# Second mixer: gate tiles through Silu on their way out of PSUM, gated and split beneath the last tiles, and the first two output tiles in the same stage

## The chip, the core and the metric

The kernel runs on one core of one Trainium2 chip. A core has a matrix engine (TensorE, PE in the rows; its weight loads are PEld), a vector engine (VectorE, DVE), an activation engine (ScalarE, ACT), GpSimd (POOL) and a sync engine that issues the DMAs (SyncE, SP). Each engine works through its own queue in order, and they meet through semaphores. The metric is the device time of one execution in microseconds; less is better.

## The reference, cut to what matters

Two blocks follow each other. The first is two layers of mixer and feed-forward and takes most of the time; the change does not touch it. The second block is one mixer layer on 512 tokens of 1024 features:

```python
proj = jnp.einsum('btd,de->bte', rmsnorm(x, pre_norm_g), w_in)
q_a, f_a, i_a, g_a, u_b, g_b, q_c, k_c, v_c, g_c, f_c = jnp.split(proj, IN_SPLIT_POINTS, axis=-1)
o_a = rmsnorm(hgrn2(silu(q_a), ...), hgrn_norm_g) * silu(g_a)   # 256 features
o_b = pooled(u_b) * pool_scale * silu(g_b)                      # 256 features
o_c = forgetting_attention(q_c, k_c, v_c, log_f_c) * silu(g_c)  # 512 features, 8 heads
mixed = jnp.concatenate([o_a, o_b, o_c], axis=-1)
y = jnp.einsum('bte,ed->btd', mixed, w_out)
out = x + rmsnorm(y, post_norm_g)
```

Everything is float32. The large products are made from parts: weight and activation are each split into a high part of type fp32r and a low rest, and three products (high by high, high by low, low by high) are summed in PSUM.

## The kernel before

The whole program is a row of stages. Each stage is one block in which every engine has its own written list of instructions; at a stage's end all engines meet (line 99), and no engine starts the next stage before all have come. The last two stages are `second_mix` and `finish`.

**`second_mix`** makes 28 dense tiles of 128 features by 512 tokens, j = 0 to 27, two for each weight unit u. Tile j is 24 matmuls: 8 slices of the contraction, kt, by 3 products. They go into the first bank of `ps0` or `ps1`. A unit of weights (1 MB) lands in one of four `raw` slots; ACT makes its high part (`split_hi`, line 158) and DVE its low part (`split_lo`, line 165) in one of two slots. The units are ordered by `SEC_COLS`: the last four units, tiles 20 to 27, are the gates g_a, g_b and g_c, and line 3574 copies these out of PSUM into `gate`, untouched.

Beneath the dense tiles lies the rest of the mixer. Behind slices 2, 5 and 7 of each tile PE calls a hook, `beside(j, x)` with x = 0, 1, 2, and ACT and DVE have the same hooks in their lists. From tile 17 on each hook holds one step i of the attention, `fox(i)`, 32 steps in all (2 groups of 4 heads, 4 chunks of queries, 4 heads). Step i on PE: the scores of i (line 3935), the transposes of the probabilities of i-1 (3945), the products with the values of i-2 (3955), and every fourth step the transposes of a finished chunk (3963). On DVE: row maximum and sum with the bias (3800), its negative (3804), every fourth step the division (3808, 3813). On ACT: the exponential of step i (3590), then the copy of the transposed probabilities of i-1 (3597), every fourth step the copy of a finished chunk into `mix` (3602). So PE needs in the next hook what ACT makes in this one. ACT's copy of a dense tile (`leave(j)`) stands behind the hook x = 2, its `split_hi` behind the hook x = 0 of every second tile, DVE's `split_lo` behind x = 1.

Tile 27 ends with step 32. Steps 33 and 34 (the `rest` list) stand behind it, then `split_hi` and `split_lo` of the second output unit and the load of ACT's function table for Silu (line 3674). The first output unit has been split in tile 26.

**`finish`** multiplies the gates by the mixer's values, splits the product into `ahi` and `alo`, multiplies by `w_out` in 8 output tiles of 24 matmuls (`one`, line 4163), takes the gain, transposes each tile to token layout (`y_turn`, 4172), and squares it for the norm; the residual `h` is transposed in 8 groups of four transposes (`h_turn`, 4154), groups 0 and 1 ahead of the tiles and six among tiles 2 to 4. For the first two tiles slices alternate between the tiles, and each slice waits for its `alo` (4115), which comes from a chain by slice: Silu on ACT (4073), product on DVE (4120), high part on ACT (4076), low part on DVE. At the end come the sums of squares (4195, 4198), the inverse root on ACT, eight fused multiply-adds (4145) and the output DMAs.

Of the kernel before, what the change touches and what calls it, by code (L numbers as in the profile page):

```python
# [23 lines left out]
P = 128  # L24
# [2293 lines left out]

def gdn(k, ins, ctx, late):
# [1093 lines left out]
def second_mix(k, cols, lower, hgrn_gain, f_cols, f_bias, pool_w, pool_scale, mix, gate, then):  # L3413
# [22 lines left out]
    with ExitStack() as ctx:  # L3436
        sb = lambda nm, shape: ctx.enter_context(nc.sbuf_tensor(f"sm_{nm}", shape, F32))
        kc = sb("kc", [P, 4, SEQ])
        ba, qa = sb("ba", [P, 4, SEQ]), sb("qa", [P, 2, SEQ])
        st, lev = sb("st", [P, 2, 2, NCH, CH]), sb("lev", [P, LEVELS, CH // 2])  # L3440
        vt, kt = sb("vt", [P, NCH, 2, P]), sb("kt", [P, 2, NCH, P])
        s2, nb = sb("s2", [P, NCH - 1, 2, P]), sb("nb", [P, FH, SEQ])
# [33 lines left out]
                 "o_ready", "inverse", "o_done", "o_turned", "out_done")  # L3476
# [21 lines left out]
        def _(sp):  # L3498
# [3 lines left out]
            with nc.allow_non_contiguous_dma(reason="256 bounds and gains, feature on partitions"):  # L3502
                sp.dma_start(lx[:, :], lower[0].rearrange("(t p) -> p t", p=P)).then_inc(s.lx_in, 16)
                sp.dma_start(hgain[:, :], hgrn_gain.rearrange("(t p) -> p t", p=P)).then_inc(s.hgain_in, 16)
            gates.sync(k, sp)
            pooling.sync(k, sp)
            for j in range(nj):
# [6 lines left out]
                if j == 9:  # L3514
                    sp.wait_ge(s.negc_out, 16)
                    sp.wait_ge(s.scanned, 1)
                    for h in range(FH):
                        sp.dma_start(nb[:, h, :], k.negc_d.ap()[h:h + 1, :].to_broadcast([P, SEQ])).then_inc(s.nb_in, 16)
            k.loaded = len(then)
# [31 lines left out]
        def _(act):  # L3551
# [3 lines left out]
            def leave(j):  # L3555
# [48 lines left out]
            def beside(j, x):  # L3604
# [44 lines left out]
                if j >= FOX0:  # L3649
                    fox(fox_at(j, x))  # L3650
            def split(j):
# [19 lines left out]
            for i in rest:  # L3671
                fox(i)
            split_hi(k, act, u0 + SECN + 1, ring(SECN + 1), t0 + nj)
            nc.scalar.preload_act_table_set("silu_and_others")

        @block.vector
        def _(dve):
# [114 lines left out]
            def fox(i):  # L3792
# [12 lines left out]
                if i % 4 == 1 and i >= 5:  # L3805
# [5 lines left out]
                    if n >= 2:  # L3811
                        dve.wait_ge(s.o_turned, n - 1)
                    dve.tensor_tensor(o[:, n % 2, :, :], bank_a[0][:, 0:4 * HW].rearrange("p (h d) -> p h d", d=HW),
                                      sm[:, n, :].unsqueeze(2).to_broadcast([P, 4, HW]), ALU.mult).then_inc(s.o_done, 1)
            def beside(j, x):
# [34 lines left out]
                if j >= FOX0:  # L3850
                    fox(fox_at(j, x))
            def split(j):
# [10 lines left out]
            for i in rest:  # L3863
                fox(i)
            split_lo(k, dve, u0 + SECN + 1, ring(SECN + 1))

        @block.tensor
        def _(pe):
# [155 lines left out]
            for i in rest:  # L4024
                fox(i)
# [5 lines left out]
def finish(k, gate, value, gain_row, out):  # L4031
# [10 lines left out]
    with ExitStack() as ctx:  # L4042
        sb = lambda nm, shape, dt=F32: ctx.enter_context(nc.sbuf_tensor(f"fin_{nm}", shape, dt))
        ahi, alo = sb("ahi", [P, KD, SEQ], F32R), sb("alo", [P, KD, SEQ], F32R)
        a, yg, sq, sqs = sb("a", [P, 2, SEQ]), sb("yg", [P, 2, SEQ]), sb("sq", [P, 2, SEQ]), sb("sqs", [P, SEQ])
        gain, rinv = sb("gain", [P, KD]), sb("rinv", [P, NCH])
        ht, yt = sb("ht", [P, NCH, D]), sb("yt", [P, NCH, D])
        names = ("gain_in", "gated", "scaled", "a_hi", "a_lo", "gained", "squared", "pooled", "y_turned", "y_out", "h_turned",
# [12 lines left out]
        def _(sp):  # L4061
            with nc.allow_non_contiguous_dma(reason="1024 gains, feature on partitions"):
                sp.dma_start(gain[:, :], gain_row.rearrange("(k p) -> p k", p=P)).then_inc(s.gain_in, 16)
# [6 lines left out]
        def _(act):  # L4070
            for kt in range(KD + 1):
                if kt < KD:
                    nc.scalar.activation(gate[:, kt, :], gate[:, kt, :], ACT.Silu).then_inc(s.gated, 1)  # L4073
                if kt > 0:
                    act.wait_ge(s.scaled, kt)
                    nc.scalar.copy(ahi[:, kt - 1, :], a[:, (kt - 1) % 2, :]).then_inc(s.a_hi, 1)  # L4076
            nc.scalar.preload_act_table_set("natural_log_exp_and_others")
# [34 lines left out]
        def _(dve):  # L4112
            def low(kt):
# [159 lines left out]
```

## Time and profile before

| | us |
|---|---|
| median of 3 runs | 1951.26 |
| lowest and highest of these | 1950.52, 1952.03 |
| the profiled execution, its own time | 1950.78 |
| its span, first to last instruction | 1949.0 |
| PE busy in the span | 1873.5 (96%) |
| DVE, ACT busy | 1058.5 (54%), 871.7 (45%) |

The rows further down come from that profiled execution, and times in them count from the start of its span. A row of a timeline gives start and duration. PE is pipelined, so its rows overlap: what a matmul costs in a stream is the distance from its start to the next one's start, not the duration in its row. A bracket at the end of a row says how long the engine had been idle before it and what ended that; a Q behind an engine's name is its sequencer, and L99 the meeting of the engines between stages.

### The profile page before, as it was taken

Reading aid. Unit: us, or ns where it says so; the run is one execution under the profiler, and the core shown is the slowest. Engines: PE = TensorE matmul, PEld = TensorE weight load, DVE = VectorE, ACT = ScalarE, POOL = GpSimd, SP = SyncE. Lnnn points to the kernel's source line nnn. Section 1 sums busy time; section 2 is a strip of 40 time slices with the busy share of each in tenths; the row PEclk is TensorE's granted clock in tenths of the full one; section 3 lists DMA queues with packets and bytes.
Section 4 is the critical chain, followed back from the end, with each engine's and each line's share of the span. In section 5 each row is a group of like instructions: output and inputs, shape, how many; then the busy total and the mean of one; then the engine's idle time right before and its main releaser. Section 6 shows DMA issues by size and latency. Waiting matters only on the chain. (4 is left out here: it accounts for less than half of the span.)

```text
span 1949.0 us, 31267 instructions
## 1 busy us (share of the span) xinstructions
PE 1873.5 (96%) x12700; PEld 1679.9 (86%) x12700; DVE 1058.5 (54%) x1724; ACT 871.7 (45%) x1449; POOL 109.4 (6%) x142
## 2 busy tenths in 40 slices
PE   7999999999899999999989999999999998999988
PEld 7999999899699999999989877788888885787666
DVE  6666599976733444444452276454443447863343
ACT  6557763667723433333343366342322333424452
POOL 0001150000000000000000020000000002001101
PEclk8999999999999999999989999999999998999989
DMA  8223362254432222322222233223223222321201
GB/s 200 85 78 126 118 191 74 62 159 138 121 92 83 87 88 94 100 87 86 86 67 88 69 78 95 87 87 108 86 90 104 86 86 67 113 66 40 65 1 44
DMA packets 209631, 179.34 MB, mean 92 GB/s; under 512 B 42544, under 2 KB 181808, under 8 KB 209512
## 3 DMA queue, kind: packets, MB, share of 16 engines
q1 hardware_dynamic: 209512, 177.68, 30.5%
q8 instruction: 83, 1.36, 0.3%
q14 instruction: 36, 0.29, 0.0%
HBM read 164.10 MB, written 13.54 MB: 91 GB/s over the span
## 5 line engine op out<-in xcount | busy, mean ns | idle before, releaser
L165 DVE TENSOR_TENSOR main_wlo<-raw,main_whi 128x2048 fp32r<-128x2048 f32 x98 | 225.7, 2303 | 328.4 <-ACT main_whi L158 328.4
L158 ACT CAST main_whi<-raw 128x2048 fp32r<-128x2048 f32 x98 | 186.5, 1903 | 368.5 <-PE ps L196 368.5
L196 PE MATMUL ps<-ffn_xhi,main_whi 128*128 128x264 f32 (+1 forms) x768 | 206.8, 323 | 6.6 <-DVE ffn_xlo L697 6.6
L196 PE MATMUL ps<-ffn_xlo,main_whi 128*128 128x264 f32 (+1 forms) x768 | 206.7, 323 | 0.0
L196 PE MATMUL ps<-ffn_xhi,main_wlo 128*128 128x264 f32 (+1 forms) x768 | 206.4, 323 | 0.0
L196 PE MATMUL ps<-ffn_alo,main_whi 128*128 128x264 f32 (+1 forms) x768 | 205.8, 322 | 0.0
L196 PE MATMUL ps<-ffn_ahi,main_wlo 128*128 128x264 f32 (+1 forms) x768 | 205.1, 321 | 0.0
L196 PE MATMUL ps<-ffn_ahi,main_whi 128*128 128x264 f32 (+1 forms) x768 | 204.7, 321 | 0.0
L196 PE MATMUL ps<-gdn_xhi,gdnf_whi 128*128 128x264 f32 x768 | 160.4, 290 | 4.2 <-DVE gdnf_wlo L1248 4.2
L196 PE MATMUL ps<-gdn_xlo,gdnf_whi 128*128 128x264 f32 x768 | 156.2, 285 | 0.0
L196 PE MATMUL ps<-gdn_xhi,gdnf_wlo 128*128 128x264 f32 x768 | 156.0, 284 | 0.0
L196 PEld LDWEIGHTS ps<-ffn_xhi,main_whi 128*128 128x128 f32 x768 | 128.9, 190 | 19.1 <-issue 7.4
L196 PEld LDWEIGHTS ps<-ffn_xlo,main_whi 128*128 128x128 f32 x768 | 128.5, 189 | 11.6 <-issue 0.2
L196 PEld LDWEIGHTS ps<-ffn_xhi,main_wlo 128*128 128x128 f32 x768 | 128.4, 190 | 11.0
L196 PEld LDWEIGHTS ps<-ffn_ahi,main_whi 128*128 128x128 f32 x768 | 127.8, 188 | 11.6
L196 PEld LDWEIGHTS ps<-ffn_alo,main_whi 128*128 128x128 f32 x768 | 127.5, 188 | 11.2
L196 PEld LDWEIGHTS ps<-ffn_ahi,main_wlo 128*128 128x128 f32 x768 | 127.5, 188 | 10.9
L380 DVE TENSOR_TENSOR h<-h,ps 128x528 f32<-128x528 f32 (+1 forms) x128 | 85.6, 691 | 81.2 <-PE ps L196 81.2
L196 PEld LDWEIGHTS ps<-gdn_xhi,gdnf_whi 128*128 128x128 f32 x768 | 120.7, 190 | 5.6 <-DVE gdn_xlo L1235 4.5
L196 PEld LDWEIGHTS ps<-gdn_xlo,gdnf_whi 128*128 128x128 f32 x768 | 119.6, 189 | 0.0
L196 PEld LDWEIGHTS ps<-gdn_xhi,gdnf_wlo 128*128 128x128 f32 x768 | 119.2, 189 | 0.0
L1137 DVE SCALAR_TENSOR_TENSOR gdn_y<-gdnf_pre,gdnf_convw,gdn_y 128x528 f32<-128x528 f32 x96 | 82.5, 861 | 59.3 <-ACT gdn_y L1110 56.9
(518 smaller groups left out, 3687.4 us busy)
## 6 DMA issues: line engine op xcount, KB each, us to landing
raw<-in_ff_up_dram SPq DMA_DIRECT2D x32, 1024.0 KB, 5.4
raw<-in_ff_down_dram SPq DMA_DIRECT2D x32, 1024.0 KB, 5.0
raw<-in_gdn_in_dram SPq DMA_DIRECT2D x24, 1024.0 KB, 5.7
raw<-in_w_in_dram SPq DMA_DIRECT2D x14, 1024.0 KB, 5.3
raw<-in_mlstm_in_dram SPq DMA_DIRECT2D x12, 1024.0 KB, 5.4
raw<-in_gdn_out_dram SPq DMA_DIRECT2D x8, 1024.0 KB, 6.6
gdn_zr<-gdn_z_spilled SPq DMA_DIRECT2D x26, 264.0 KB, 3.2
gdn_v_spilled<-gdn_o SPq DMA_DIRECT2D x16, 264.0 KB, 2.2
```

The source lines that it names most:

```text
L158: k.nc.scalar.copy(k.whi[:, slot % SPLIT_SLOTS, :], k.raw[:, slot, :]).then_inc(k.hi_done, 1)
L165: eng.tensor_tensor(k.wlo[:, s, :], k.raw[:, slot, :], k.whi[:, s, :].bitcast(F32), ALU.subtract).then_inc(k.lo_done, 1)
L196: mm = pe.matmul(ps[:, b, 0:k.width], w, x[:, half], start=first and n == 0, stop=last and n == 2)
L380: dve.tensor_tensor(parted(k, acc[:, j, k.now]), parted(k, acc[:, j, k.now]), filled(k, k.ps[j % 4]), ALU.add).then_inc(s.down_free, 1)
L1137: dve.scalar_tensor_tensor(out=self.y[:, b, :], in0=self.pre[:, b, i:i + T], scalar=self.w[:, i, j:j + 1], in1=self.y[:, b, :], op0=ALU.mu ...
```

## The change

Four things are done together.

1. Tiles 20 to 27 leave PSUM through Silu instead of a copy. Silu lives in another function table than Exp and Ln, so a load of the table stands ahead of each Silu and another behind it.
2. The product with the mixer's values, the high part and the low part of slices 0 to 5 are made beneath the tiles that follow: for slice kt the product stands on DVE behind the hook x = 0 of tile 21 + kt, the high part on ACT behind x = 1, the low part on DVE behind x = 2. Slices 6 and 7 stand at the stage's end. The results lie in two buffers (`fin_first`, `fin_second`) placed over scratch of the stage that is free by then (`under_both`, `Gated`).
3. The first two output tiles move into `second_mix`, behind tile 27: slices 0 to 5 of tile 0, with steps 33 and 34 of the attention behind its slices 2 and 5, slices 0 to 5 of tile 1, then slices 6 and 7 of both.
4. `finish` starts with output tile 2. All eight groups of `h_turn` now stand among tiles 2 to 5. The DMA of the gains moves to the start of `second_mix`; the two table loads (lines 3674 and 4077) are gone.

```diff
@@ second_mix, SyncE
+                sp.dma_start(out_gain[:, :], gain_row.rearrange("(k p) -> p k", p=P)).then_inc(s.gain_in, 16)
@@ second_mix, ScalarE
-                    ins = nc.scalar.copy(gate[:, 2 * (u - 10) + m, :], src)
+                    ins = nc.scalar.activation(gate[:, j - SEC_GATE0, :], src, ACT.Silu)
                 ins.then_inc(s.left, 1)
+                if j >= SEC_GATE0:
+                    nc.scalar.preload_act_table_set("natural_log_exp_and_others")
+            def gated_high(kt_):
+                act.wait_ge(s.gated, kt_ + 1)
+                nc.scalar.copy(gated.hi(kt_), gate[:, kt_, :]).then_inc(s.gated_hi, 1)
...
+                if x == 1 and SEC_GATE0 < j <= SEC_GATE0 + 6:
+                    gated_high(j - SEC_GATE0 - 1)
...
             for i in rest:
                 fox(i)
+            for kt_ in range(6, KD):
+                gated_high(kt_)
             split_hi(k, act, u0 + SECN + 1, ring(SECN + 1), t0 + nj)
-            nc.scalar.preload_act_table_set("silu_and_others")
@@ second_mix, VectorE
+            def gated_product(kt_):
...
+                dve.wait_ge(s.left, SEC_GATE0 + kt_ + 1)
+                g = gate[:, kt_, :]
+                dve.tensor_tensor(g, g, mix[:, kt_, :], ALU.mult).then_inc(s.gated, 1)
+            def gated_low(kt_):
+                dve.wait_ge(s.gated_hi, kt_ + 1)
+                dve.tensor_tensor(gated.lo(kt_), gate[:, kt_, :], gated.hi(kt_).bitcast(F32), ALU.subtract)\
+                    .then_inc(s.gated_lo, 1)
...
+            gated_product(6)
+            gated_product(7)
+            gated_low(6)
+            gated_low(7)
             split_lo(k, dve, u0 + SECN + 1, ring(SECN + 1))
@@ second_mix, TensorE
-            for i in rest:
-                fox(i)
+            pe.wait_ge(k.lo_done, u0 + SECN + 1)
+            after = {2: rest[0], 5: rest[1]}
+            for j in range(2):
+                pe.wait_ge(s.left, nj - 1 + j)
+                for kt_ in range(6):
+                    pe.wait_ge(s.gated_lo, kt_ + 1)
+                    gated.tile(k, pe, j, kt_, u0 + SECN, dense[j])
+                    if j == 0 and kt_ in after:
+                        fox(after[kt_])
+            for kt_ in range(6, KD):
+                pe.wait_ge(s.gated_lo, kt_ + 1)
+                for j in range(2):
+                    gated.tile(k, pe, j, kt_, u0 + SECN, dense[j])
@@ finish, TensorE
-            for g in range(2):
-                h_turn(g)
-            pe.wait_ge(k.lo_done, u0 + 1)
-            for kt in range(KD):
-                pe.wait_ge(s.a_lo, kt + 1)
-                for j in range(2):
-                    one(j, kt)
             for j in range(2, 2 * n):
...
-                    if j < 5 and kt in (2, 5):
-                        h_turn(2 * (j - 1) + (2, 5).index(kt))
+                    if j < 6 and kt in (2, 5):
+                        h_turn(2 * (j - 2) + (2, 5).index(kt))
```

The order on PE where the two stages meet, before. `sm_ba` holds probabilities, `sm_qa` their transposes, `sm_s2` a finished chunk, `h` the residual:

```order
L196 MATMUL ps1<-sec_xhi,main_wlo 128x512
L3945 MATMUL ps2<-ident,sm_ba 128x128
L3955 MATMUL ps0<-sm_vt,sm_qa 128x64 x2
L3963 MATMUL ps1<-ident,sm_s2 128x128 x2
L99 UNCONDITIONAL_BRANCH
L4148 UNCONDITIONAL_BRANCH
L4154 MATMUL ps2<-ident,h 128x128 x4
L4154 MATMUL ps3<-ident,h 128x128 x4
L4163 MATMUL ps0<-fin_ahi,main_whi 128x512
```

The same place on PE in the change, from the last dense tile's end through the first six matmuls of output tile 0 and the step behind them:

```order
L196 MATMUL ps1<-sec_xhi,main_wlo 128x512
L4017 MATMUL ps2<-ident,sm_ba 128x128
L4027 MATMUL ps0<-sm_vt,sm_qa 128x64
L3443 MATMUL ps0<-fin_first,main_whi 128x512 x2
L3443 MATMUL ps0<-fin_first,main_wlo 128x512
L3443 MATMUL ps0<-fin_first,main_whi 128x512 x2
L3443 MATMUL ps0<-fin_first,main_wlo 128x512
L3443 MATMUL ps0<-fin_first,main_whi 128x512 x2
L3443 MATMUL ps0<-fin_first,main_wlo 128x512
L4027 MATMUL ps0<-sm_vt,sm_qa 128x64
```

The second product with the values moved behind nine matmuls, the transposes of the last chunk behind nine more, and the residual's transposes behind the meeting of the engines.

The order on ACT around the end of tile 26 (x = 2 there and x = 0 in tile 27), before:

```order
L3590 ACTIVATE sm_ba,wide<-sm_ba,wide 128x128
L3597 COPY sm_qa<-ps2 128x128
L3574 COPY wide<-ps0 128x512
L3590 ACTIVATE sm_ba,wide<-sm_ba,wide 128x128
L3597 COPY sm_qa<-ps2 128x128
L3602 COPY wide<-ps1 128x2x128
```

and in the change:

```order
L3634 ACTIVATE sm_ba,wide<-sm_ba,wide 128x128
L3641 COPY sm_qa<-ps2 128x128
L3613 ACT_TABLE_LOAD
L3613 ACTIVATE wide<-ps0 128x512
L3616 ACT_TABLE_LOAD
L3634 ACTIVATE sm_ba,wide<-sm_ba,wide 128x128
L3641 COPY sm_qa<-ps2 128x128
L3646 COPY wide<-ps1 128x2x128
```

Two loads now stand between the exponential of one hook and that of the next. On DVE the stage's end reads, in the change:

```order
L3855 RECIPROCAL wide<-wide 128x4
L3860 TENSOR_TENSOR sm_s2<-ps0,wide 128x256
L3874 TENSOR_TENSOR wide<-wide 128x512 x2
L3877 TENSOR_TENSOR fin_first<-wide,fin_first 128x512 x2
L165 TENSOR_TENSOR main_wlo<-raw,main_whi 128x2048
L99 UNCONDITIONAL_BRANCH
```

The low part of the weights (line 165) now stands behind the products and low parts of slices 6 and 7.

## Rows read from the trace of the kernel before

**Rows 1.** The page: busy time, share and instructions of each engine

```profile
PE 1873.5 (96%) x12700; PEld 1679.9 (86%) x12700; DVE 1058.5 (54%) x1724; ACT 871.7 (45%) x1449; POOL 109.4 (6%) x142
```

**Rows 2.** The chain that ended last, in `finish`: start, us, what

```profile
1885.68 15.84 PE ps L4163 x57
1901.52 0.44 PE ps L4154 x4
...
1904.93 3.50 PE ps L4163 x15
```

**Rows 3.** Timeline of PE from tile 27's last matmul to output tile 2

```profile
1875.66 0.39 PE L196 MATMUL ps<-sec_xhi,main_wlo 128*128 128x512 f32 x1
...
1877.53 0.44 PE L3963 MATMUL ps<-ident,sm_s 128*128 128x128 f32 x2 [0.57 <-DVE sm_s L3813]
1882.83 1.94 PE L4154 MATMUL ps<-ident,h 128*128 128x128 f32 x8 [4.86 <-PEq L99]
1885.68 0.76 PE L4163 MATMUL ps<-fin_ahi,main_whi 128*128 128x512 f32 x1 [0.92 <-DVE fin_alo L4115]
...
1899.26 0.40 PE L4163 MATMUL ps<-fin_ahi,main_whi 128*128 128x512 f32 x1
```

**Rows 4.** Timeline of ACT and DVE over the same seam

```profile
1876.20 0.27 ACT L3597 COPY sm_qa<-ps 128x128 f32<-128x128 f32 x1 [0.80 <-PE ps L3945]
...
1878.01 0.37 ACT L3602 COPY wide<-ps 128x256 f32<-128x256 f32 x1 [1.05 <-PE ps L3963]
1878.28 1.90 ACT L158 CAST main_whi<-raw 128x2048 fp32r<-128x2048 f32 x1
...
1880.21 2.29 DVE L165 TENSOR_TENSOR main_wlo<-raw,main_whi 128x2048 fp32r<-128x2048 f32 x1 [2.74 <-ACT main_whi L158]
...
1883.47 1.29 DVE L4120 TENSOR_TENSOR fin_a<-wide 128x512 f32<-128x512 f32 x2 [0.97 <-ACT wide L4073]
...
1884.19 0.62 ACT L4076 CAST fin_ahi<-fin_a 128x512 fp32r<-128x512 f32 x1 [0.24 <-DVE fin_a L4120]
...
1884.85 0.69 DVE L4115 TENSOR_TENSOR fin_alo<-fin_a,fin_ahi 128x512 fp32r<-128x512 f32 x1
```

**Rows 5.** Windows; behind the busy times stands PEclk, the granted clock

```profile
1885.60:1890.80 5.20, 5.12 (x12) 4.08 (x13) 4.84 (x8) 4.46 (x9) 0.00 (x0) 0.50 0.00 0
1890.80:1899.30 8.50, 8.50 (x38) 6.83 (x38) 5.35 (x9) 3.46 (x5) 0.00 (x0) 1.00 0.00 0
```

**Rows 6.** Timeline of PE at an earlier meeting of the engines

```profile
1202.30 0.39 PE L196 MATMUL ps<-mls_xhi,main_wlo 128*128 128x512 f32 x1
1203.02 0.70 PE L196 MATMUL ps<-mls_early,main_whi 128*128 128x512 f32 x2 [0.32 <-PEq L99]
1203.56 0.40 PE L196 MATMUL ps<-mls_early,main_wlo 128*128 128x512 f32 x1
```

**Rows 7.** Timeline of ACT around a table load for Silu, tile 4

```profile
1657.35 0.72 ACT L3376 ACTIVATE sm_nb<-sm_nb,ones 8x512 f32<-8x512 f32 x1
1658.09 1.28 ACT L3564 ACT_TABLE_LOAD   x1
1659.38 0.60 ACT L3564 ACTIVATE sm_qa<-ps 128x512 f32<-128x512 f32 x1
```

**Rows 8.** Timeline of ACT and PE between tiles 26 and 27

```profile
1868.93 0.58 ACT L3574 COPY wide<-ps 128x512 f32<-128x512 f32 x1
1871.60 0.40 ACT L3590 ACTIVATE sm_ba<-sm_ba,wide 128x128 f32<-128x128 f32 x1 [2.08 <-DVE wide L3804]
...
1874.12 0.33 PE L3945 MATMUL ps<-ident,sm_ba 128*128 128x128 f32 x1
...
1874.43 0.48 PE L196 MATMUL ps<-sec_xhi,main_whi 128*128 128x512 f32 x1
...
1874.75 0.39 PE L196 MATMUL ps<-sec_xlo,main_whi 128*128 128x512 f32 x1
```

**Rows 9.** Timeline of ACT and PE between tiles 22 and 23, widest steps

```profile
1825.13 0.58 ACT L3574 COPY wide<-ps 128x512 f32<-128x512 f32 x1
1827.55 0.72 ACT L3590 ACTIVATE sm_ba<-sm_ba,wide 128x512 f32<-128x512 f32 x1 [1.83 <-DVE wide L3804]
...
1831.31 0.66 PE L3945 MATMUL ps<-ident,sm_ba 128*128 128x128 f32 x4
```

More of the change, by code:

```diff
@@ L2316, in under, with under_both @@
         return t
+def under_both(k, first, second):
+    with k.nc.sbuf_tensor(*first, F32) as a, k.nc.sbuf_tensor(*second, F32) as b:
+        return a, b
 def gdn(k, ins, ctx, late):
@@ L3410, in second_unit, with __init__, room, hi @@
     return lambda u: tall(ins["w_in_2"][0], SEC_COLS[u])
-def second_mix(k, cols, lower, hgrn_gain, f_cols, f_bias, pool_w, pool_scale, mix, gate, then):
+class Gated:
+    def __init__(self, gate, value, first, second):
+        self.gate, self.value, self.first, self.second = gate, value, first, second
+    def room(self, kt, part):
+        if 4 <= kt < 6:
+            return self.second[:, 2 * (kt - 4) + part, :]
+        return self.first[:, 2 * (kt if kt < 4 else kt - 2) + part, :]
+    def hi(self, kt):
+        return self.room(kt, 0)
+    def lo(self, kt):
+        return self.room(kt, 1)
+    def tile(self, k, pe, j, kt, u0, bank):
+        u, m = u0 + j // 2, j % 2
+        x, cols = u % RAW_SLOTS % SPLIT_SLOTS, slice(m * P, (m + 1) * P)
+        whi = k.whi[:, x, :].rearrange("p (k n) -> p k n", k=KD)
+        wlo = k.wlo[:, x, :].rearrange("p (k n) -> p k n", k=KD)
+        for i, (w, y) in enumerate(((whi, self.hi(kt)), (whi, self.lo(kt)), (wlo, self.hi(kt)))):
+            mm = pe.matmul(bank, w[:, kt, cols], y, start=kt == 0 and i == 0, stop=kt == KD - 1 and i == 2)
+        if kt == KD - 1:
+            mm.then_inc(k.tile_full, 1)
+SEC_GATE0 = 20
+def second_mix(k, cols, lower, hgrn_gain, f_cols, f_bias, pool_w, pool_scale, mix, gate, st, nb, kt, kc, gated, out_gain,
+               gain_row, then):
     nc = k.nc
@@ L4028, in second_mix, with finish @@
     k.split = 2
-def finish(k, gate, value, gain_row, out):
+def finish(k, gated, gain, out):
     nc = k.nc
@@ L4070, in _ @@
         def _(act):
[L4071 to L4077, printed above, removed]
             def square(j):
@@ L4214, in second @@
                        w[:, 3584:3584 + FH], ins["fox_f_bias_2"][0], ins["pool_w_2"][0], ins["pool_scale_2"][0], mix, gate,
+                       st, nb, kt, kc, gated, gain, ins["post_norm_g_2"][0],
                        [tall(ins["w_out_2"][0], 256 * u) for u in range(4)])
-        finish(k, gate, mix, ins["post_norm_g_2"][0], out)
+        finish(k, gated, gain, out)
 _USED = ["x", "meta_tokens", "attn_norm", "ffn_norm", "ff_up", "ff_down", "gdn_in", "gdn_conv", "gdn_a_log",
```

67 lines of the change are left out of this document (29 added, 38 removed).

## The prediction

> **What bounds the kernel now.** The page comes first: PE is busy 96% of the span and no other engine over 54% [rows 1], so time goes away only where PE stands still, or runs below full speed, and an engine that gets more work costs nothing while PE does not wait for it. The chain of waits is read next for the stretch that the change touches: in `finish` it is nothing but PE's matmuls from 1885.68 on, 57 of them in 15.84 us [rows 2], so every microsecond by which this stream starts earlier ends the kernel earlier. Then the timeline of PE ahead of that chain. Tile 27's last matmul starts at 1875.66, output tile 2's first at 1899.26, 23.60 us later [rows 3]. Between them lie 48 matmuls of output tiles 0 and 1. In a stream of full speed 15 such matmuls take 3.50 us, 0.233 us each [rows 2], so 48 are 11.20 us. Half of the 23.60 us is something else, and the rows name it: 4.86 us idle until the engines meet, 0.92 us idle until the first slice's low part is there [rows 3], and a granted clock of 0.50, the 1.2 GHz level, until about 1890.8. The 12 matmuls in that window took 5.20 us and not 2.80, which is 2.4 us lost; from there on the clock is 1.00, 2.4 GHz [rows 5]. Ahead of the fall PE had stood for most of 5 us.
>
> What ends last at that meeting is DVE: `split_hi` 1.90 us, then `split_lo` 2.29 us until 1882.50 [rows 4]. Both belong to output tiles 2 and 3, which PE does not need yet.
>
> **The change, part by part.**
>
> *PE between 1875.66 and output tile 2.* In the change this reads: the last dense matmul 0.23; the small group of step 32; nine matmuls, the values of step 31, nine more, the transposes of the last chunk, 18 of tile 1, 12 of slices 6 and 7; the meeting of the engines. A small group costs, from its first row to the dense matmul behind it, 1874.43 - 1874.12 = 0.31 us, and the dense matmul then 0.32 rather than 0.23 [rows 8], so 0.40. Three of them are 1.20 us. The seam: where all other engines had come before PE, 0.72 us lay between the two matmuls' starts around the meeting [rows 6], 0.49 above a stream's 0.23. Sum: 0.23 + 1.20 + 11.20 + 0.49 = 13.12 us against 23.60. That is 10.48 us less, if PE waits for nothing and the clock stays.
>
> *The residual's transposes.* Groups 0 and 1 stood in time that was lost anyway; now they stand in PE's stream, 0.44 us each [rows 2]: 0.88 us more.
>
> *Does PE wait for the gated slices?* Slices 0 to 5 have their low parts one tile after their gates left, the last in tile 26; PE wants them after tile 27. Slices 6 and 7 are the narrow place. Their product needs the last chunk. By the sum above its transposes end at about 1881.3 on PE. Then, with durations from [rows 4]: copy on ACT 0.37 (1881.7); two products on DVE 1.29 (the first at 1882.4, both at 1883.0); high parts on ACT 0.62 each (1883.1, 1883.7); low parts on DVE 0.69 each, by about 1883.8 and 1884.5. PE wants slice 6 after 18 more matmuls, at about 1885.4, and slice 7 1.4 us later. The slack is 1.6 us; without that cover PE would stand 4 us there. The clock should stay up, since PE never stands for over half a microsecond.
>
> *Do the engines meet in time?* `split_hi` follows the high parts, 1883.7 + 1.90 = 1885.6, `split_lo` 2.29 more: 1887.9. PE's last matmul of slice 7 starts at about 1888.0 and the engines meet behind its end. DVE is there 0.3 us before PE. This is the thinnest cover; gone, it costs only what DVE is late.
>
> *What ACT pays for Silu.* Each gate tile's exit was a copy of 0.58. Now it is a load, Silu, a load. The trace has such a load beside its Silu: the load starts as the instruction before ends, takes 1.28 us, and Silu from PSUM starts 0.01 us behind it and takes 0.60 [rows 7]. So an exit takes 1.28 + 0.60 + 1.28 + 0.03 = 3.2 us instead of about 0.5, eight times, with a high part of 0.62 more in six of the tiles. Over 20 us more on ACT, all beneath PE's tiles, and the question is whether any of it reaches PE. Behind the exit of tile 26 ACT had 2.08 us idle until the next exponential [rows 8]. Exit from 1869.0 to 1872.2 puts that exponential 0.6 us late, its end with the copy behind it at 1872.8. PE wants it at 1874.12: slack 1.3 us. At the widest steps, behind tile 22, the exit would end at 1828.4, the exponential 0.9 us late, exponential and two copies done by 1830.2, and PE wants them from 1831.31 on [rows 9]: slack 1.1 us. The others lie between or better. I take 0 for the tiles; the upper bound is the rival below.
>
> *DVE's products and low parts* (0.69 each, six pairs) fall into idle time like the 2 us that [rows 8, 9] show on ACT; each follows the attention's step of its hook. Behind it only the next hook's step is queued, about 3 us later.
>
> *The DMA of the gains* moves ahead of the attention's gate weights and the pooling weights on SP; a 4 KB transfer, first used by PE two tiles later. 0.
>
> *`finish`* begins with gain, square and `split_hi` for output unit 2 as soon as the engines have met; its low part is wanted two tiles (over 13 us) later. 0.
>
> Sum: 10.48 - 0.88 = 9.6 us less. On the profiled execution's own 1950.78 us that is 1941.2. That execution lies 0.5 below the median of 1951.26; halfway between them, since the three runs themselves spread over 1.5 us, I say **1941.4 us**.
>
> **The rivals.**
>
> *A, the seam is not clean.* The low parts of slices 6 and 7 come later than PE, or DVE's `split_lo` makes the meeting late, PE stands, and the clock falls once more. Price: the standing (1 to 2 us) and the 2.4 us of the half clock [rows 5]. Gain 5 to 6: 1945.2. Against it: 1.6 us of slack, and a meeting of 0.72 us left the clock at full rate [rows 6].
>
> *B, a table switch costs more than its load.* If ACT lost a further 1.4 us per load, which the rows do not show (Silu 0.01 us behind the load [rows 7]), an exit would take 6.0 us. Behind tile 26 the exponential would start at 1875.0 instead of by 1874.12 less its 0.40: PE stands 1.3 us there, and by the same working 0 to 1.5 us behind the other six exits that a hook follows, some 6.5 us in all. Gain 3: 1948.0. The Trainium skill, "ScalarE: Activation LUTs", section "What ACT_TABLE_LOAD costs", gives each switch a load of about 1283 ns and on top of it a drain of about 1380 ns, 2.66 us in all; by that rule B is the forecast. The trace agrees on the load's length and shows no drain.
>
> *C, slower than before.* ACT's lateness reaches PE at the exits, and each time PE slows to 1.2 GHz for a stretch like that of [rows 5]: 2.4 us and the standing, some 3 us for each of the seven exits that a hook follows. It decides from the fourth exit on (9.6 / 3 = 3.2); all seven would be 21 us, 1962. For it: the work is put on ACT at seven places. Against it: it needs ACT over 1.1 us later than worked out at the tightest place, and pauses of a fraction of a microsecond between hooks do not lower the clock today.
>
> *D, it does not do what it says:* slices 0 to 5 are not ready beneath the tiles (a product waits for its gate tile with the attention's steps queued behind it on DVE), and the idle time only moves ahead of tile 27. Gain under 4: 1949.
>
> **How the numbers follow.** Forecast 0.80, A 0.08, B 0.06, C 0.03, D 0.03. Range 1939.8 to 1945.2: below, a seam and small groups at half their price (1 us) and the runs' own spread; above, A. A measurement of this kernel can tell about 0.2%, 3.9 us, from no change. Forecast and A are faster by more than that (0.88). B, 3.3 us below the median, and D lie within it, though B's sum is soft enough to put 0.02 of it on the faster side. C is slower: faster 0.90, same 0.07, slower 0.03.
>
> **What would show it.** Right: PE's row of output tile 2's first matmul 9 to 11 us earlier (near 1888.8), granted clock 1.00 through the seam, Exp rows behind the exits starting at most 1 us later while PE's transposes stay where they were. Wrong: a bracket with ACT or DVE on PE's rows in tiles 21 to 27 (B, C, D), a gap of over 1.5 us ahead of slice 6 or at L99 and matmuls 0.43 us apart behind it (A). A drain would be a gap between a load's end and the exponential behind it.

## The result, and the profile after

The changed kernel took **1935.88 us** (median of 4 runs, 1935.70 to 1939.68); the kernel before, in its runs beside it, 1950.89 (4 runs, 1949.47 to 1952.03). The ratio is 0.9928, 95% interval 0.9911 to 0.9945. The direction was forecast; the time lies 5.5 us below the forecast and 3.9 us below the range's low end. With all the runs of the experiments the picture changes: 26 runs of the changed kernel have a mean of 1939.8 us (1935.55 to 1947.63), 104 of the kernel before 1949.5 (1943.31 to 1957.31). The difference of the means is 9.8 us, with two standard errors 8.3 to 11.2. The four runs of the result lie low: of the other 22 runs of the same kernel only one is below 1935.88, and four drawn at random from all 26 have so low a median about once in 170.

The profiled execution after took 1935.70, its span is 1934.0, 15.0 shorter than before. First PE's line of the page, which answers [rows 1]: 7.1 us less busy. Of that 2.4 are the matmuls at the seam, which no longer run at 1.2 GHz, and 2.9 lie ahead of the second mixer (1565.5 us busy before, 1562.6 after), where nothing was changed.

```profile
PE 1866.4 (97%) x12700; PEld 1674.9 (87%) x12700; DVE 1059.8 (55%) x1724; ACT 886.6 (46%) x1455; POOL 107.0 (6%) x142
```

The timeline of PE from tile 27's last matmul to output tile 2, which answers [rows 3]; columns as there (L4017 are turns of probabilities, L4027 values, L4035 the chunk's transposes, L3443 the output tiles):

```profile
1870.60 0.39 PE L196 MATMUL ps<-sec_xhi,main_wlo 128*128 128x512 f32 x1
1870.83 0.27 PE L4017 MATMUL ps<-ident,sm_ba 128*128 128x128 f32 x1
...
1871.08 0.71 PE L3443 MATMUL ps<-fin_first,main_whi 128*128 128x512 f32 x2
1871.63 0.39 PE L3443 MATMUL ps<-fin_first,main_wlo 128*128 128x512 f32 x1
...
1873.26 0.33 PE L4027 MATMUL ps<-sm_vt,sm_qa 128*128 128x64 f32 x2
1873.40 0.72 PE L3443 MATMUL ps<-fin_first,main_whi 128*128 128x512 f32 x2
1873.95 0.39 PE L3443 MATMUL ps<-fin_first,main_wlo 128*128 128x512 f32 x1
...
1880.02 0.63 PE L3443 MATMUL ps<-fin_first,main_whi 128*128 128x512 f32 x2
...
1881.41 0.63 PE L3443 MATMUL ps<-fin_first,main_whi 128*128 128x512 f32 x2
...
1882.58 0.40 PE L3443 MATMUL ps<-fin_first,main_wlo 128*128 128x512 f32 x1
1883.30 0.70 PE L3443 MATMUL ps<-fin_first,main_whi 128*128 128x512 f32 x2 [0.33 <-PEq L99]
```

From 1870.60 to 1883.30 are 12.70 us; before they were 23.60, forecast were 13.12. The one bracket is the meeting of the engines, 0.33 us. The windows of this stretch and the next (PEclk is the third number from the right) answer [rows 5]:

```profile
1870.60:1883.30 12.70, 12.38 (x57) 9.74 (x56) 5.30 (x6) 6.83 (x8) 0.00 (x0) 1.00 0.00 0
1883.30:1890.80 7.50, 7.50 (x39) 6.18 (x40) 5.04 (x6) 3.58 (x4) 1.30 (x1) 1.00 0.01 2
```

The granted clock is 1.00 through the seam. ACT and DVE over the same stretch, which answers [rows 4]: tile 27's exit (load, Silu, load), the last chunk's copy, products, high and low parts of slices 6 and 7, and the split of output unit 2.

```profile
1871.42 1.28 ACT L3613 ACT_TABLE_LOAD   x1
1872.71 0.60 ACT L3613 ACTIVATE wide<-ps 128x512 f32<-128x512 f32 x1
1873.33 1.28 ACT L3616 ACT_TABLE_LOAD   x1
1876.01 0.37 ACT L3646 COPY wide<-ps 128x256 f32<-128x256 f32 x1 [1.39 <-PE ps L4035]
...
1876.41 1.29 DVE L3874 TENSOR_TENSOR wide<-wide 128x512 f32<-128x512 f32 x2 [2.30 <-ACT wide L3646]
1877.79 1.29 DVE L3877 TENSOR_TENSOR fin_first<-wide,fin_first 128x512 fp32r<-128x512 f32 x2
1880.20 2.29 DVE L165 TENSOR_TENSOR main_wlo<-raw,main_whi 128x2048 fp32r<-128x2048 f32 x1 [1.11 <-ACT main_whi L158]
```

The row of low parts (L3877) holds two of 0.69 us each: that of slice 6 is there at 1878.5, that of slice 7 at 1879.1. PE takes slice 6 at 1880.02 and slice 7 at 1881.41: 1.5 and 2.3 us of slack. DVE ends at 1882.49, and PE starts its last matmul ahead of the meeting at 1882.58. Last, ACT and PE behind the exit of tile 26, which answers [rows 8] and, for the load and its Silu, [rows 7]:

```profile
1864.19 1.28 ACT L3613 ACT_TABLE_LOAD   x1
1865.48 0.60 ACT L3613 ACTIVATE wide<-ps 128x512 f32<-128x512 f32 x1
1866.10 1.28 ACT L3616 ACT_TABLE_LOAD   x1
1867.39 0.40 ACT L3634 ACTIVATE sm_ba<-sm_ba,wide 128x128 f32<-128x128 f32 x1
...
1869.04 0.33 PE L4017 MATMUL ps<-ident,sm_ba 128*128 128x128 f32 x1
```

The exponential starts 0.01 us behind the second load. ACT takes its next copy into `mix` at 1867.94, 1.1 us before PE turns the result. At the widest steps, behind tile 22 [rows 9], the exponential starts at 1823.35, it and two copies are done at 1824.9, and PE wants them from 1826.21 on: 1.3 us.

**Where the 15.0 us of span lie.** Four stretches, whose ends are rows of the timelines: the start of the second mixer (its first DMA), tile 27's last matmul, the first transpose of the residual inside output tile 2 (2.1 to 2.2 us behind that tile's first matmul), and the span's end.

```profile
1619.36 0.37 SPq L3503 DMA_DIRECT2D sm_lx<-in_lower_bounds_dram  x1
```

```profile
1614.79 0.37 SPq L3540 DMA_DIRECT2D sm_lx<-in_lower_bounds_dram  x1
```

The first row is of before, the second of after. Before, the ends lie at 1619.36, 1875.66, 1901.36, 1949.0; after, at 1614.79, 1870.60, 1885.48, 1934.0. So 4.57 us were gained ahead of the second mixer, where nothing was changed; 0.49 in its tiles; 10.82 at the seam; and 0.88 were lost behind it. The edited part gives 9.94 us. The other 5.06 are the question.

### The profile page after: what moved, and what is told of

The parts are those of the page before. It is cut to its first block and busy times, and to the rows that moved or that the text cites. A ratio compares the mean times of both kernels' runs of the same rounds, so it can differ in the third digit from the quotient of the medians.

```text
span 1934.0 us, 31276 instructions
## 1 busy us (share of the span) xinstructions
PE 1866.4 (97%) x12700; PEld 1674.9 (87%) x12700; DVE 1059.8 (55%) x1724; ACT 886.6 (46%) x1455; POOL 107.0 (6%) x142
## 5 line engine op out<-in xcount | busy, mean ns | idle before, releaser
L196 PEld LDWEIGHTS ps<-ffn_ahi,main_whi 128*128 128x128 f32 x768 | 128.0, 188 | 11.6
L196 PEld LDWEIGHTS ps<-ffn_alo,main_whi 128*128 128x128 f32 x768 | 126.9, 188 | 11.2
```

Of the source, the lines that this page charges most:

```text
L196: mm = pe.matmul(ps[:, b, 0:k.width], w, x[:, half], start=first and n == 0, stop=last and n == 2)
```

## The experiments

Theory L (chance): the unchanged stages take another time in each execution, and the result caught a short one. Rival P (program): the changed program really speeds up what lies ahead of it. The runs were made in four groups, each on one chip and beside runs of the kernel before: same_before, same_after, beneath_only and extra_loads; same_before2, same_after2, silu_only and one_load; same_after3 and tail_split; one_extra. The ratios compare within a group.

### Both kernels again, unedited

> The kernel before, unchanged, run and profiled again. The two first profiles differ by 15.0 us in span, but only 9.9 us of that lie between tile 27's last matmul and the end; 4.6 us are there already when second_mix begins (engines released at 1619.2 us before, 1614.6 after), in stages whose code the change leaves alone. Theory L (lottery): those 4.6 us are a matter of the single execution, mostly of how long TensorE happens to be at 1.2 GHz in the earlier stages (34 us of such stretches before, 24 us after); this profile's second_mix then begins anywhere within 1614 to 1620 us and the times of this kernel spread over several us. Theory P (program): they belong to the program as built; second_mix begins at 1619 +- 1 us again and the median is 1951 +- 1 us.

> The changed kernel, unchanged, run and profiled again. Theory L (lottery): second_mix begins anywhere within 1614 to 1620 us, and the difference to the kernel before comes out nearer to 9.9 us than to 15. Theory P (program): second_mix begins at 1614.6 +- 1 us again, the median is 1936 +- 1 us and the difference is 15 us. Under both, the stretch from tile 27's last matmul to output tile 2's first takes 12.7 us and the stretch from there to the end 50.7 us.

> The changed kernel once more, nothing edited. Theory L (the local gain is fixed, about 9.9 us from tile 27's last matmul to the end, and what a single run shows beside that is chance in the stages that the change leaves alone): from tile 27's last dense matmul to output tile 2's first 12.70 us again within 0.1 and from there to the end of the span 50.7 within 0.3; median of the runs 1940 to 1943, ratio to before 0.994 to 0.996; the start of the second mixer anywhere between 1614 and 1621. Theory P (the changed program also speeds up what comes ahead of it, by code or buffers that lie elsewhere): median 1935 to 1937, start of the second mixer at 1615 or below.

> The kernel before once more, nothing edited. Theory L: the runs again spread over more than 8 us with a mean of 1949 to 1951, the long ones with the lower mean clock, about 1.5 us for each 0.001 (26 runs of it gave a slope of 1.45 us, correlation -0.84); from the last dense matmul to output tile 2's first 23 to 24 us. Theory P: second mixer's start at 1618 to 1620 every time.

> The changed kernel, nothing edited, as the neighbour of the version with the split tail and for more runs of it. From tile 27's last dense matmul to output tile 2's first 12.70 us, from there to the end 50.7; median 1938 to 1943; over all its runs and all of before's, means 9 to 11 us apart.

| run | median us (n) | ratio to before, 95% | mixer starts | last dense matmul | seam | behind it |
|---|---|---|---|---|---|---|
| before, first profile | | | 1619.36 | 1875.66 | 25.70 | 47.64 |
| same_before | 1948.03 (10) | 1.0002, 0.9988 to 1.0016 | 1617.78 | 1873.22 | 25.31 | 47.67 |
| same_before2 | 1948.69 (12) | 0.9997, 0.9984 to 1.0011 | 1618.99 | 1874.74 | 25.36 | 47.70 |
| after, first profile | 1935.88 (4) | 0.9928, 0.9911 to 0.9945 | 1614.79 | 1870.60 | 14.88 | 48.52 |
| same_after | 1941.94 (5) | 0.9959, 0.9941 to 0.9978 | 1618.98 | 1875.45 | 14.88 | 48.47 |
| same_after2 | 1939.45 (7) | 0.9956, 0.9938 to 0.9974 | 1617.11 | 1872.93 | 14.88 | 48.49 |
| same_after3 | 1938.84 (10) | 0.9950, 0.9935 to 0.9966 | 1621.10 | 1877.46 | 14.88 | 48.46 |

"Seam" is from tile 27's last matmul to the residual's transpose in tile 2, "behind it" from there to the end. These two columns repeat to 0.06 us within a kernel, before's seam apart (0.4). The start of the mixer moves over 1614.8 to 1621.1 with the same program, so P, which put it at 1615 or below every time, falls: the gain at the seam is the same in the slowest and in the fastest of these profiles, and the 4.57 us ahead of it come and go. L stands. From the mixer's start to the last dense matmul are 255.4 to 256.3 us in the three profiles of before and 255.8 to 256.5 in the four of the changed kernel, so the tiles with their new exits give nothing and cost at most some tenths. Of the numbers expected, the median of 1940 to 1943 for same_after2 missed (1939.45); the 23 to 24 us of same_before2 held (25.36 - 2.10 = 23.26), and the mean of its runs, 1949.2, fits.

What moves is in part the clock. Over the 67 runs of the kernel before in three of the groups the mean granted clock lay between 0.978 and 0.987; 15 runs at 0.982 had a mean of 1951.8 us, 10 at 0.985 one of 1946.7. The line through all has 1.2 us for each 0.001 (1.5 were expected), correlation -0.78. That is not all of it. Ahead of the mixer the records show 37.5 us at the half clock in before's first profile and 30.4 in after's; at half speed those 7.1 us cost 3.6 at most, of the 4.57. But over all 13 profiles of this study, in which this time was 30.4 to 47.5 us, the mixer's start follows it only loosely (correlation 0.47): same_after3, with 34.1, starts last. In before's and after's first profiles a part of the difference also stands as 0.13 us in each turn of the first block's first feed-forward loop, 23.49 against 23.36, at a granted clock of 1.00 in both; that is 1.3 us over ten turns. All 13 profiles have one of these two values. The changed kernel has 23.36 in three of its profiles and 23.49 in same_after3, silu_only has 23.36, and before had 23.49 in all three of its own. So it is not fixed by the program; what makes it was not found and stays open.

### The change without PE's new order

Everything of the change, but output tiles 0 and 1 stay in `finish`:

```diff
@@ second_mix, TensorE
-            after = {2: rest[0], 5: rest[1]}
-            for j in range(2):
...
-                    gated.tile(k, pe, j, kt_, u0 + SECN, dense[j])
+            for i in rest:
+                fox(i)
@@ finish, TensorE
-            for j in range(2, 2 * n):
+            for j in range(2 * n):
```

> The change without its third part: Silu at the exits and products, high and low parts beneath the tiles, but output tiles 0 and 1 stay at the start of finish, as whole tiles one after the other. Theory M (the gain is the overlap of the output tiles with the seam): the engines meet when DVE's split of the second output unit ends, which now stands behind the products of slices 6 and 7; about 9 us after tile 27's last matmul, and output tiles 0 and 1 follow with some 12 matmuls at 1.2 GHz. Worked out: 9.2 + 11.2 + 2.4 = 22.8 us from tile 27's last matmul to output tile 2's first, against 23.6 before and 12.7 in the change, so a gain of 0 to 1 us locally. Rival: the gated operands being ready is worth the most of the gain, then this is 5 us or more faster than before locally. For the rest of the difference: theory L lets second_mix begin anywhere in 1614 to 1620 us, theory P has it as the program decides, and this is another program than both.

Measured: 1952.08 us (10 runs), ratio 1.0007, 0.9996 to 1.0018; no gain. The timeline of PE, and of ACT and DVE behind tile 27's last matmul (1876.46), shows where it went:

```profile
1887.29 1.19 PE L3443 MATMUL ps<-fin_first,main_whi 128*128 128x512 f32 x2 [8.53 <-PEq L99]
```

```profile
1877.28 1.28 ACT L3613 ACT_TABLE_LOAD   x1
1878.57 0.60 ACT L3613 ACTIVATE wide<-ps 128x512 f32<-128x512 f32 x1
1879.19 1.28 ACT L3616 ACT_TABLE_LOAD   x1
1880.48 0.37 ACT L3646 COPY wide<-ps 128x256 f32<-128x256 f32 x1
...
1884.67 2.29 DVE L165 TENSOR_TENSOR main_wlo<-raw,main_whi 128x2048 fp32r<-128x2048 f32 x1 [1.10 <-ACT main_whi L158]
```

The exit of 3.2 us, the gating of slices 6 and 7 and the split stand one behind the other, and PE stands for all of it, 8.53 us in a piece. The engines meet 10.8 us behind the last dense matmul, where 9.2 were expected: that sum had no exit in it. Output tile 2 starts 23.6 us behind the last dense matmul (expected 22.8, before 23.2 to 23.6). The gain of the change is the cover that the 48 matmuls give. The work put beneath the tiles gains nothing by itself; it is what lets slices 0 to 5 stand in that place.

### The gate tiles' exits alone

The kernel before with the Silu exits, and without the eight Silus in `finish`:

```diff
@@ second_mix, ScalarE
-                    ins = nc.scalar.copy(gate[:, 2 * (u - 10) + m, :], src)
+                    ins = nc.scalar.activation(gate[:, 2 * (u - 10) + m, :], src, ACT.Silu)
                 ins.then_inc(s.left, 1)
+                if u >= 10:
+                    nc.scalar.preload_act_table_set("natural_log_exp_and_others")
...
-            nc.scalar.preload_act_table_set("silu_and_others")
@@ finish, ScalarE
-                    nc.scalar.activation(gate[:, kt, :], gate[:, kt, :], ACT.Silu).then_inc(s.gated, 1)
```

> The kernel before with one part of the change alone: the eight gate tiles leave through Silu with the table put back behind each, and the finish stage no longer begins with eight Silus; PE's order, the gating, the splits and all output tiles stay where they were. If the exits cost PE nothing and the finish's entry waited for the Silus only once (the first Silu is 0.60 us, behind it DVE's product, the split and PE's first output matmul), it gains 0.6 us: last dense matmul to output tile 2's first 22.9 us against 23.6, and a time within 0.05% of before. Rival (the gain lies in taking the Silus off ACT, each of the eight on the path): 8 x 0.6 = 4.8 us, 1945. Rival (each exit pushes PE): slower by 3 us or more, with PE idle behind the turn copies in tiles 20 to 27.

Measured: 1948.98 us (10 runs), ratio 0.9995, 0.9985 to 1.0005. The time cannot tell it from before; the rows can, and they say 0.9 us worse: from the last dense matmul (1874.79) to the residual's transpose in tile 2 26.23 us against 25.31 and 25.36 of the two repeats of before. My 0.6 us of gain was there and something larger stood against it:

```profile
1877.52 1.28 ACT L3577 ACT_TABLE_LOAD   x1
...
1879.08 1.90 ACT L158 CAST main_whi<-raw 128x2048 fp32r<-128x2048 f32 x1
...
1883.63 1.94 PE L4150 MATMUL ps<-ident,h 128*128 128x128 f32 x8 [6.54 <-PEq L99]
1885.85 0.76 PE L4159 MATMUL ps<-fin_ahi,main_whi 128*128 128x512 f32 x1 [0.28 <-DVE fin_alo L4112]
```

Tile 27's exit now stands ahead of the split, so the engines meet 8.84 us behind the last dense matmul and not 7.17 as in [rows 3] (1882.83 - 1875.66); behind the meeting the first slice comes sooner (2.22 us against 2.85). In tiles 20 to 27 PE waited for no exit, so the rival that each exit pushes PE falls, and so does the one that the eight Silus of `finish` stand on the path (1945).

### How much slack an exit has

Two further table loads ahead of each Silu of a gate tile, then one:

```diff
+                    nc.scalar.preload_act_table_set("silu_and_others")
+                    nc.scalar.preload_act_table_set("natural_log_exp_and_others")
                     ins = nc.scalar.activation(gate[:, j - SEC_GATE0, :], src, ACT.Silu)
```

> The change with two more function table loads ahead of each gate tile's Silu, 2.57 us more on ACT at each of eight exits. Theory M: ACT's lateness was 0.5 to 1 us and its slack about 1.1 us, so now PE has to stand at six of the seven exits that a hook follows: 1.2, 0.95, 0.5, 0, 0.55, 1.2 and 1.35 us, and 0.7 us at the meeting of the engines; 6.5 us slower than the change, and the granted clock stays at 1.00 in tiles 21 to 27. Rival C of the prediction: each standing takes the clock down for a stretch, 3 us each, 15 us or more slower. Rival: if a load cost ACT 1.4 us more than its row, this would be 12 us slower or more.

Measured: 1951.67 us (10 runs), ratio 1.0004, 0.9993 to 1.0016. The whole gain is gone. Behind six of the seven exits that a hook follows PE stands ahead of the turn of the probabilities, five times by 1.03 to 1.27 us and last by 2.58, 8.5 us in all. Below stand three of these rows and two windows, the granted clock again the third number from the right:

```profile
1859.03 0.44 PE L4019 MATMUL ps<-ident,sm_ba 128*128 128x128 f32 x2 [1.22 <-ACT sm_ba L3636]
1870.63 0.44 PE L4019 MATMUL ps<-ident,sm_ba 128*128 128x128 f32 x2 [1.24 <-ACT sm_ba L3636]
1882.38 0.47 PE L4019 MATMUL ps<-ident,sm_ba 128*128 128x128 f32 x1 [2.58 <-ACT sm_ba L3636]
```

```profile
1840.00:1860.00 20.00, 18.78 (x97) 13.14 (x95) 8.40 (x22) 18.62 (x29) 2.28 (x5) 1.00 0.17 54
1882.40:1887.40 5.00, 5.00 (x15) 4.12 (x16) 0.18 (x1) 2.15 (x7) 0.00 (x0) 0.50 0.00 0
```

The expectation missed twice: 6.5 us of standing were expected, and a clock of 1.00 in these tiles. Behind the five pauses of 1.03 to 1.27 us it did stay at 1.00. In the last one it fell, and it stood at 0.50 from 1881.7 to 1888.5; of that PE worked 6.1 us, which at half speed cost up to 3.1. With the 8.5 that makes 11.6, and the means of the runs lie 11.8 apart (1951.6 and 1939.8).

This is rival B's mechanism, put in by hand: the price per switch decides the change. The Trainium skill, "ScalarE: Activation LUTs", section "What ACT_TABLE_LOAD costs", puts a drain of about 1380 ns on top of each load. Two switches per exit would by that figure be an estimated 2.8 us more, close to the 2.6 us that this kernel adds. The trace of after disagrees with a drain: Silu and the exponential stand 0.01 us behind their loads, and the loads 0.02 us behind what is ahead of them.

> The changed kernel with one further table load (1.29 us) ahead of each Silu of a gate tile. With two further loads, 2.58 us, PE stood 1.03 to 1.27 us in tiles 21 to 26, so the slack of an exit is 1.3 to 1.55 us there, and one load more should just fit: PE idle in tiles 21 to 26 under 0.1 us each, the seam 0 to 0.5 us longer (ACT's last exit stands in front of chunk 1's copy, the product and the low parts of slices 6 and 7, which were done 0.9 us ahead of PE), median as the changed kernel within 1 us. If instead the delay were queueing on ACT in proportion to its load, half the loads would cost half the stall, 0.5 to 0.6 us per tile and 4 us in all: 1946.

That edit did nothing: the added line named the table that Silu loads itself, and ACT's rows show one load ahead of Silu, as in the changed kernel. Its 1939.15 us (4 runs), 0.9943, 0.9923 to 0.9962, and its seam of 14.88 are those of the changed kernel once more and say nothing of slack. With another table it is a load more:

```diff
+                    nc.scalar.preload_act_table_set("sigmoid_and_others")
                     ins = nc.scalar.activation(gate[:, j - SEC_GATE0, :], src, ACT.Silu)
```

> The changed kernel with truly one more table load ahead of each Silu of a gate tile (the table of the sigmoid; in the run one_load the added line named the table that the Silu loads itself, so it added nothing). An exit of 3 x 1.28 + 0.60 = 4.5 us. Slack reading: two more loads, 2.58 us, made PE stand 1.03 to 1.27 us, so the slack is 1.3 to 1.55 us and 1.29 us just fits: PE idle behind the turn copies under 0.1 us each in tiles 21 to 26; tile 27's own exit ends at about 5.1 us behind the last matmul where the chunk's transposes end at 5.3, so the seam stays 12.7 us, 12.9 at most; median 1938.5 to 1941. Proportional reading (half the loads, half the stall): 0.5 to 0.6 us per tile, 4 us in all and 0.7 more at the seam, 1944.

Measured: 1944.27 us (8 runs), ratio 0.9965, 0.9945 to 0.9985. The slack reading missed its numbers: 1938.5 to 1941 was expected, and 12.7 to 12.9 us from the last dense matmul to output tile 2. By the median alone the proportional reading would have won (1944). The rows say otherwise: PE stands at no exit of tiles 20 to 25, and once, behind tile 26, for 1.32 us.

```profile
1865.69 1.90 ACT L158 CAST main_whi<-raw 128x2048 fp32r<-128x2048 f32 x1
...
1867.62 2.29 DVE L165 TENSOR_TENSOR main_wlo<-raw,main_whi 128x2048 fp32r<-128x2048 f32 x1 [1.45 <-ACT main_whi L158]
1869.83 0.29 DVE L3848 CUSTOM_DVE_ANT_0 sm_ba<-ps,sm_nb 128x128 f32<-128x128 f32 x1
...
1870.35 0.40 ACT L3635 ACTIVATE sm_ba<-sm_ba,wide 128x128 f32<-128x128 f32 x1 [1.59 <-DVE wide L3852]
...
1871.01 1.28 ACT L3613 ACT_TABLE_LOAD   x1
...
1876.05 0.33 PE L4018 MATMUL ps<-ident,sm_ba 128*128 128x128 f32 x1 [1.32 <-ACT sm_ba L3635]
```

Ahead of it lies a chain that I had not followed: tile 25's late exit makes `split_hi` late, that makes `split_lo` late on DVE, behind it the next step's maximum is queued, and that makes the next exit late. So this exit starts 0.50 us before the turn of the step ahead (1871.51) and not 1.69 before it (1865.88) as in the changed kernel. 1.19 us came through the chain, and 1.29 is its own; against a slack of 1.10 that makes 1.38, and 1.32 were seen. The clock fell 1.1 us behind the pause's end and was back 3.4 us later, 0.71 on average over the window from the pause's end on, although pauses of 1.03 to 1.27 us had left it at 1.00 in extra_loads. The stretch from the last dense matmul to output tile 2's first took 13.81 us, not 12.70:

```profile
1876.05:1882.00 5.95, 5.95 (x23) 4.79 (x23) 0.18 (x1) 3.87 (x9) 0.00 (x0) 0.71 0.00 0
```

### Beyond the change: the last eight pieces on two engines

Behind PE's last instruction DVE makes the result alone. Two of its eight pieces went to ACT (scale) and GpSimd (sum):

```diff
@@ finish, ScalarE
+                nc.scalar.activation(sq[:, p, :], yt[:, c, x], ACT.Copy, scale=rinv[:, c:c + 1]).then_inc(s.scaled, 1)
@@ finish, GpSimd
+            for p, i in enumerate(by_pool):
+                x, c = pieces[i]
+                pool.wait_ge(s.scaled, p + 1)
+                pool.tensor_tensor(ht[:, c, x], sq[:, p, :], ht[:, c, x], ALU.add).then_inc(s.made_pool, 1)
@@ finish, VectorE
+                if i in by_pool:
+                    continue
```

> A version beyond the change. Behind PE's last instruction (1925.24 us in the changed kernel's profile) DVE makes the eight pieces of the result alone, 8 x 0.67 = 5.39 us, then the last write lands. Here two of the eight (pieces 3 and 5) are made by ACT (scaled by the row's factor, about 0.6 us each) and GpSimd (the sum, about 1.3 us each), DVE keeps six: 6 x 0.67 = 4.0 us. If DVE's row is the tail and GpSimd runs beside it, the stretch from PE's last y turn to the end of the span falls from 8.8 to 7.4 us; the median falls by 1.3 us against the changed kernel, less than the runs' scatter, so the rows decide. Rival (GpSimd and DVE slow each other, or the sum takes 2 us): 0 to 0.5 us gained. Rival (ACT's scaled copy in front of the last y copy, 0.6 us, holds DVE's later pieces back): slower by 0.3 us or less, with DVE idle ahead of the fourth piece.

Measured: 1940.34 us (8 runs), ratio 0.9958, 0.9943 to 0.9973, no better than the changed kernel beside it (1938.84). The groups of the last stretch, columns as in the page's part 5, first of the changed kernel, then of this one:

```profile
L4204 DVE SCALAR_TENSOR_TENSOR fin_ht<-fin_yt,fin_rinv,fin_ht 128x512 f32<-128x512 f32 x8 | 5.4, 745 | 1.2 <-ACT fin_rinv L4171 1.2
```

```profile
L4221 DVE SCALAR_TENSOR_TENSOR fin_ht<-fin_yt,fin_rinv,fin_ht 128x512 f32<-128x512 f32 x6 | 6.1, 1080 | 1.2 <-ACT fin_rinv L4175 1.2
L4197 POOL TENSOR_TENSOR fin_ht<-fin_sq,fin_ht 128x512 f32<-128x512 f32 x2 | 3.3, 1690 | 6.8 <-ACT fin_sq L4182 6.8
```

Six pieces take DVE longer (6.1 us) than eight did (5.4). The mean of 1080 ns hides two sorts. By the view of line 4221 alone the six take 740 ns at least, 748 in the median and 1756 at most: the four that GpSimd does not hold up take about 745, as in the changed kernel, and the two that run with GpSimd's sums about 1750. GpSimd's sum takes 1690 where the same form took 1290 in the tiles (line 4182). The stretch from the last y turn to the end is 9.95 us against 8.76, where 7.4 were expected. The rival with the two engines in each other's way had the mechanism and was still too mild; it is a loss.

## Why the prediction was right in kind and wrong in size

**What bounds the kernel: right.** PE's stream behind tile 27 sets the end; the change without PE's new order gains nothing. One reading was loose: the clock at the old seam did not fall behind most of 5 us of standing. It fell at 1880.5, 2.5 us into the pause, and was back at 1890.75, as [rows 5] say.

**PE between 1875.66 and output tile 2: forecast 13.12, measured 12.70.** The 0.23, the 48 matmuls at 0.233 and the seam's 0.49 hold. Three small groups at 0.40 were too dear: from the first row of a group to the third matmul behind it are 0.80 us (1870.83 to 1871.63), 0.69 and 0.69, less 0.47 for two matmuls of the stream: 0.33 + 0.22 + 0.22 = 0.77, not 1.20. That is the 0.42. I had taken the price of a group with turns and values; one that is only values, or only the chunk's transposes, costs about half.

**The residual's transposes: forecast +0.88.** From output tile 2's first matmul to the end the span took 49.74 us before and 50.70 after, +0.96. The sum, 9.6 us, stands against 9.94 in the first pair of profiles, 9.6 to 10.0 over all pairs of the seven in the table, and 9.8 (8.3 to 11.2) between the means of all runs.

**Slices 6 and 7: right.** The low part of slice 6 was there 1.5 us before PE wanted it, forecast 1.6: both came some 0.3 us sooner than worked out. **The meeting:** DVE 0.1 us before PE's last matmul, forecast 0.1; 0.72 us between the matmuls around it, as in [rows 6].

**ACT's exits: right.** 3.2 us each, no drain, and PE waits for none. Behind tile 26 the forecast slack was 1.3 us, the trace shows 1.1; behind tile 22 forecast 1.1, shown 1.3. What I had missed shows only in one_extra: the lateness of an exit is handed on through the splits to the next, so the slacks of two exits are not independent. With the change's own exits it costs nothing.

**The rivals.** A (a seam that is not clean) and B (a drain) did not occur: clock 1.00 and 0.01 us. What B and C would have cost shows in extra_loads, whose exits (5.8 us) are nearly as long as B's (6.0). B had put the standing at 6.5 us and left the clock alone; it was 8.5, and the clock took up to 3.1 more. C had a fall of the clock behind each of seven exits; it came behind one, the pause of 2.58 us, and in one_extra behind the one pause of 1.32. D would have shown PE idle ahead of slices 0 to 5; there is none.

**The step that failed** is the last one, the range: "below, a seam and small groups at half their price (1 us) and the runs' own spread". Below the forecast the range had 1.6 us, 1 for the first term and 0.6 for the spread. I had sized it by three runs that lay within 1.5 us. Among 26 runs of the kernel before on one chip the spread was 14 us (1943.31 to 1957.31), their standard deviation 3 us; three runs drawn from these lie within 1.5 us of each other only once in 10 times. The base was off with it: 1950.78 and 1951.26 stand for a mean of 1949.5, which moves the forecast by 1.5 us. With my 9.6 us off that mean one gets 1939.9, next to my low end, and 15 of 26 runs of the changed kernel lie below 1939.8. So even a hit would have been half luck. The remaining 4.0 us to 1935.88 lie in the four runs of the result, whose mean granted clock was 0.987 to 0.988; of the other 22 runs only one had over 0.987, and it took 1935.55. Four such runs together are unlikely by chance (once in 170), and no run shows whether it was chance or something of the chip that they ran on. An honest range for the same sum would have been 1939.9 and two standard deviations of 3 us either way, an estimate of about 1934 to 1946. The page of before held a warning that I did not use, its row of the granted clock in 40 slices:

```profile
PEclk8999999999999999999989999999999998999989
```

Four slices stand at 8, two of them far ahead of the second mixer, and [rows 5] show what one stretch at the half clock costs, 2.4 us. A few such stretches more or less per execution were to be expected.

## What to carry to other kernels

Moving work beneath another engine's tiles gained nothing by itself here; what gained was PE work placed over the serial chain at a stage's end. The exits alone, and the exits with the gating, gave no gain; PE's new order was not run without them, since its slices 0 to 5 need the gated parts. Follow a late instruction through the splits and the next hook's queue before you call its slack free. And size the range by the spread of many runs or of the clock rows, not by three runs that happen to agree: here a local sum good to 0.3 us was put beside a base whose single runs have a standard deviation of 3.

## What the runs showed of the hardware

- The same program's span moved by up to 14 us of 1950 on one chip; 0.001 of mean granted clock went with 1.2 us. The edited stretches of the changed kernel repeated to 0.06 us in the same executions.
- An exponential behind a table load started 0.01 us after it, with two loads around the Silu; with three, at most 0.02 us.
- A table load whose table is the one that the next instruction needs replaces that instruction's own load and costs nothing (one_load).
- A scalar-tensor-tensor on DVE, 128x512, took 745 ns alone and about 1750 when it ran with GpSimd's sum; that sum took 1690 ns, and 1290 in the tiles.
- The length of a pause alone did not tell whether the granted clock fell. It fell 1.5, 1.9 and 2.5 us into pauses of 8.53, 2.58 and 4.86 us (beneath_only, extra_loads, before), and 1.1 us behind the end of one of 1.32 us (one_extra); five pauses of 1.03 to 1.27 us (extra_loads) and the 0.33 us at the meeting left it at 1.00.
- The same loop at a granted clock of 1.00 took 23.49 us a turn in seven profiles and 23.36 in six, the same program in both sorts.
